# The last four experts of a mixture layer, one by one instead of side by side

## The reference

```python
# mixture: group of 8 experts by argmax, two of its experts, weights from the softmax
weights = p_g * top_p / jnp.sum(top_p, axis=-1, keepdims=True)
...
    a = jax.nn.silu(xb @ w_gate_e[e]) * (xb @ w_up_e[e])     # w_gate_e, w_up_e: 32 x 1024 x 256
    return a @ w_down_e[e]                                     # w_down_e: 32 x 256 x 1024
...
y = yb.reshape(R, D) * row_w[:, None].astype(yb.dtype)
out = jax.ops.segment_sum(y, row_tok, num_segments=T + 1)[:T]
# after it: x = x + out; x = rms_norm(x, final_norm_g), then the second block:
h = rms_norm_2(x, g_pre_mix[i])
q, k, v = split_heads(h, w_qkv)
```

## Time and profile before

| | |
|---|---|
| median of 3 runs | 795.57 us (794.38 to 796.18) |
| profiled execution | 795.36 us, its span 793.6 us |
| TensorE busy | 740.5 us, 93% of the span |
| VectorE busy | 417.3 us, 53% |
| ScalarE busy | 332.8 us, 42% |
| DMA, mean over the span | 257 GB/s, near 420 GB/s in the expert stage |

### The profile page before, as it was taken

How to read it: one execution, slowest core, us unless ns; L and a number is a source line. 1 busy time by engine, 2 the same in 40 slices (tenths; PEclk the granted TensorE clock), 3 DMA queues, 4 the chain that set the end, 5 groups by cost and what they waited for, 6 DMA issues and landing times.

```text
span 793.6 us, 12361 instructions
## 1 busy us (share of the span) xinstructions
PE 740.5 (93%) x5110; PEld 611.7 (77%) x5110; DVE 417.3 (53%) x740; ACT 332.8 (42%) x594; POOL 30.9 (4%) x64
## 2 busy tenths in 40 slices
PE   8999999999999999998776769999998999999996
PEld 8899898888788876665444539899877888888885
DVE  3747756676767421110110107665658776777665
ACT  4667465545444421110110117565556444344442
POOL 0600000000000000000000001000002000000000
PEclk9999999999999999999988989999999999999999
DMA  8765486456978999999999999954433475555201
GB/s 315 273 182 158 146 284 227 171 173 207 371 263 314 341 379 421 420 420 422 421 421 420 421 394 355 374 182 157 145 125 112 151 250 174 170 202 180 87 0 54
DMA packets 83850, 203.97 MB, mean 257 GB/s; under 512 B 6992, under 2 KB 47824, under 8 KB 71248
## 3 DMA queue, kind: packets, MB, share of 16 engines
q1 hardware_dynamic: 83792, 203.15, 69.1%
HBM read 202.09 MB, written 1.05 MB: 256 GB/s over the span
## 4 chain that ended last, share of the span: by engine, by line
PE 80%; DMA 11%; ACT 3%; DVE 3%; SPq 2%; issue 1%; DVEq 0%; ACTq 0%
PE ps L622 44%; PE ps L690 9%; PE ps L953 5%; PE ps L693 5%; DMA big<-in_w_gate_e 4%; DMA ext<-in_w_up_e 3%; DMA raw<-in_w_gate_e 3%; PE ps L974 2%; PE ps L932 2%; PE ps L984 2%; SPq L467 1%; DVE wl L1563 1%; PE ps L585 1%; ACT junk L1191 1%; PE ps L1039 1%
## 5 line engine op out<-in xcount | busy, mean ns | idle before, releaser
L1563 DVE TENSOR_TENSOR wl<-raw,wh 128x1024 fp32r<-128x1024 f32 (+3 forms) x180 | 213.1, 1199 | 130.7 <-ACT wh L1182 129.2
L1182 ACT CAST wh<-raw 128x1024 fp32r<-128x1024 f32 (+3 forms) x180 | 181.8, 1028 | 66.7 <-PE ps L622 46.3
L622 PE MATMUL ps<-wh,fra 128*128 128x512 f32 (+3 forms) x668 | 189.5, 369 | 1.1 <-DVE wl L1563 0.7
L622 PEld LDWEIGHTS ps<-wh,fra 128*128 128x128 f32 x668 | 118.6, 189 | 20.1 <-DVE wl L1563 1.7
L622 PE MATMUL ps<-wl,fra 128*128 128x512 f32 (+3 forms) x334 | 121.3, 363 | 0.0
L690 PE MATMUL ps<-fra,wh 128*128 128x512 f32 x352 | 110.6, 396 | 0.0
L622 PE MATMUL ps<-fra,wh 128*128 128x256 f32 x464 | 86.1, 287 | 1.4 <-DVE big L1984 1.4
L693 PEld LDWEIGHTS ps<-fra,wl 128*128 128x128 f32 x352 | 66.1, 188 | 15.5
L622 PEld LDWEIGHTS ps<-fra,wh 128*128 128x128 f32 x464 | 72.7, 192 | 2.4 <-issue 2.2
L622 PE MATMUL ps<-wh,frb 128*128 128x512 f32 x240 | 74.3, 391 | 0.0
L622 PEld LDWEIGHTS ps<-wl,fra 128*128 128x128 f32 x334 | 62.9, 188 | 9.7
(11 more groups left out here) (245 smaller groups left out, 920.4 us busy)
## 6 DMA issues: line engine op xcount, KB each, us to landing
raw<-in_w_gate_e SPq DMA_DIRECT2D x28, 1024.0 KB, 23.9
ext<-in_w_up_e SPq DMA_DIRECT2D x24, 1024.0 KB, 26.4
raw<-in_w_in SPq DMA_DIRECT2D x16, 1024.0 KB, 5.2
ext<-in_w_down_e SPq DMA_DIRECT2D x16, 1024.0 KB, 24.2
raw<-in_w_qkv SPq DMA_DIRECT2D x12, 1024.0 KB, 12.8
raw<-in_w_gate SPq DMA_DIRECT2D x11, 1024.0 KB, 5.3
raw<-in_w_up SPq DMA_DIRECT2D x11, 1024.0 KB, 5.2
raw<-in_w_down SPq DMA_DIRECT2D x11, 1024.0 KB, 4.9
```

The lines of the kernel that those rows point to most:

```text
L622: t = e.matmul(o, a, w, start=first and n == 0, stop=final and n == 2, skip_group_check=not check)
L1182: e.copy(halves(q)[0], piece_view(q)).then_inc(*up("wh", q))
L1563: e.tensor_tensor(l, piece_view(q), h.bitcast(F), ALU.subtract).then_inc(*up("wl", q))
```

## The change

Group 7 alone is done in another way; groups 0 to 6 are as before.

- The combine weights of group 7 are made and turned during group 6, after its combine (`select_last_weights`, `gather_last_weights`), and lie four times over, once on each 32 partitions, in `CM7`, one tile for each of the four experts.
- Between the gate and the up product of group 7 stand 26 filler products.
- `one_expert(j)` then takes the four experts in turn. Down product: the 32 slots of one expert go to four groups of 32 partitions of one bank, and each group gets another quarter of the 1024 features. ScalarE alone copies the bank (128x256). Combine: eight products, each with 32 rows of the array (one group), into `turned(k)`. After the first three experts stand three filler products; the 12 are gone.
- `combined` for the eight tiles is now raised in the last four products of the last expert.
- The second block's first unit, ("q", 0), is fetched as two units of half a megabyte. The gains, and then the bias table, come one whole unit earlier in the queue.

```diff
-WARM = (15, 3, 12, 9, 14, 4)
+WARM = (15, 3, 3, 9, 14, 4, 26)
...
-            wt.split((key, c), w_qkv[0].rearrange("(k p) n -> p k n", p=P)[:, :, col:col + 256])
+            w = w_qkv[0].rearrange("(k p) n -> p k n", p=P)[:, :, col:col + 256]
+            wt.split((key, c), *((w[:, 0:4], w[:, 4:8]) if (key, c) == ("q", 0) else (w,)))
...
+    last_weighed = big[:, 1280:1792]
...
+    YE7 = [junk[:, 256 * j:256 * j + 256] for j in range(4)]
+    CM7 = [ext[:, 8, 256 * j:256 * j + 256] for j in range(4)]
...
             for half_, key in enumerate(("eg", "eu")):
+                if half_ and g == 7:
+                    warm(WARM[6], 3)
...
-        def experts_down(g):
+        def turn_hidden(g):
             z = g % 2
...
-            if g == 7:
-                warm(WARM[2], 3)
+
+        def experts_down(g):
+            z = g % 2
+            turn_hidden(g)
...
+        def gather_last_weights():
+            for r in range(2):
+                enter(1, "CM", 7, r)
+                e.wait_ge(*at("sel weights", 7, r))
+                for n in range(4):
+                    t = e.transpose(bank[1][:, P * n:P * n + P], last_weighed[:, P * n:P * n + P], ident)
+                t.then_inc(*up("CM turned", 7, r))
+
+        def one_expert(j):
+            b, ed = 2 + j % 2, wt.raws["ed", 28 + j]
+            e.wait_ge(*landed(ed))
+            enter(b, "YE act", 7, j)
+            for k in range(2):
+                for r in range(4):
+                    t = e.matmul(bank[b][32 * r:32 * r + 32, 0:256], AT[1][:, P * k + 32 * j:P * k + 32 * j + 32],
+                                 slot_view(ed)[:, k, 256 * r:256 * r + 256], start=(k == 0), stop=(k == 1))
+            t.then_inc(*(up("taken", "ed", 7) if j == 3 else up("down", 7, j)))
+            e.wait_ge(*at("YE act", 7, j))
+            for s in range(2):
+                for r in range(4):
+                    k, rows = 2 * r + s, slice(32 * r, 32 * r + 32)
+                    t = e.matmul(turned(k), YE7[j][rows, P * s:P * s + P], CM7[j][rows, :], start=False, stop=(j == 3),
+                                 skip_group_check=True)
+                    if j == 3 and s:
+                        t.then_inc(*up("combined", 7, k))
+            if j < 3:
+                warm(WARM[2], 0)
...
             experts(g)
-            gather_weights(g)
             if g < 7:
+                gather_weights(g)
                 gather(g + 1)
-            experts_down(g)
-            combine(g)
+                experts_down(g)
+                combine(g)
+            if g == 6:
+                gather_last_weights()
+        turn_hidden(7)
+        e.wait_ge(*at("AT", 7))
+        for j in range(4):
+            one_expert(j)
...
+            if g == 6:
+                for r in range(2):
+                    e.wait_ge(*at("CM turned", 7, r))
+                    e.copy(ext[:, 8, 512 * r:512 * r + 512], bank[1][:, :]).then_inc(*up("CM", 7, r))
+        for j in range(4):
+            e.wait_ge(*(at("taken", "ed", 7) if j == 3 else at("down", 7, j)))
+            e.copy(YE7[j], bank[2 + j % 2][:, 0:256]).then_inc(*up("YE act", 7, j))
...
+        def select_last_weights():
+
+            e.wait_ge(*at("gathered", 7, 1))
+            slots = C[:, C_IOTA:C_IOTA + CAP].unsqueeze(1).to_broadcast([P, 4, CAP])
+            for r in range(2):
+                e.wait_ge(*(at("CM turned", 7, 0) if r else at("CM turned", 6)))
+                for n in range(4):
+                    j, i = 2 * r + n // 2, n % 2
+                    t = e.tensor_scalar(last_weighed[:, P * n:P * n + P].rearrange("p (e s) -> p e s", e=4), slots,
+                                        PX[:, i, 28 + j:29 + j], kept_W[:, i, 28 + j:29 + j], ALU.is_equal, ALU.mult)
+                t.then_inc(*up("sel weights", 7, r))
```

More of the change, by code:

```diff
@@ L983, in combine @@
                     e.wait_ge(*at(("YE act", "YE dve")[k // 4], g))
-                t = e.matmul(turned(k), YE[k // 4][:, P * (k % 4):P * (k % 4) + P], CM, start=False, stop=(g == 7),
+                t = e.matmul(turned(k), YE[k // 4][:, P * (k % 4):P * (k % 4) + P], CM, start=False, stop=False,
                              skip_group_check=True)
-                if g == 7 and k % 2:
-                    t.then_inc(*up("combined", g, k))
-            if g < 7:
-                t.then_inc(*up("combined", g))
+            t.then_inc(*up("combined", g))
+        def gather_last_weights():
[24 more added lines that the diff above has]
+                warm(WARM[2], 0)
         gather(0)
@@ L1429, in scalar @@
             e.activation(AE[z], bank[0][:, 0:256], ACT.Silu).then_inc(*up("expert silu", g))
-            e.wait_ge(*at("CM turned", g))
-            e.copy(CM, bank[1][:, 0:256]).then_inc(*up("CM", g))
             if g < 7:
+                e.wait_ge(*at("CM turned", g))
+                e.copy(CM, bank[1][:, 0:256]).then_inc(*up("CM", g))
                 gather(g + 1)
@@ L1435, in scalar @@
             e.copy(AT[z], bank[1][:, 0:256]).then_inc(*up("AT", g))
-            e.wait_ge(*at("down", g))
-            e.copy(YE[0], bank[2][:, :]).then_inc(*up("YE act", g))
+            if g < 7:
+                e.wait_ge(*at("down", g))
+                e.copy(YE[0], bank[2][:, :]).then_inc(*up("YE act", g))
+            if g == 6:
[5 more added lines that the diff above has]
+            e.copy(YE7[j], bank[2 + j % 2][:, 0:256]).then_inc(*up("YE act", 7, j))
         if real:
@@ L1958, in vector @@
             e.tensor_tensor(AE[z], AE[z], bank[0][:, 256:512], ALU.mult).then_inc(*up("expert a", g))
+            if g < 6:
+                select_weights(g + 1)
             if g < 7:
-                select_weights(g + 1)
                 gather(g + 1)
-            e.wait_ge(*at("taken", "ed", g))
-            e.tensor_copy(YE[1], bank[3][:, :]).then_inc(*up("YE dve", g))
+                e.wait_ge(*at("taken", "ed", g))
+                e.tensor_copy(YE[1], bank[3][:, :]).then_inc(*up("YE dve", g))
+            if g == 6:
+                select_last_weights()
         if real:
@@ L2107, in general_vector @@
     def general_vector(e):
-        e.wait_ge(*at("YE act", 7))
+        e.wait_ge(*at("YE act", 7, 3))
         e.wait_ge(*at("combined", 7, 7))
```

## The result

The changed kernel took **802.12 us** (median of 4 runs, 799.28 to 803.46) against 795.70 us for the kernel before on the same chip: a ratio of 1.0073, 95% interval 1.0059 to 1.0087, so 0.7% slower. The forecast was slower by 3 us, 798.7 us, range 796.0 to 802.5; the sign and the mechanism hold, the size is about double. The profiled execution took 799.28 us, its span 797.5 us.

The account below looks back on a forecast made before the run. The prediction took as bound when ScalarE can begin the eight high halves. Up product -2.3 us, spent at once; last expert's result +3.6, pacing -0.35: +3.2 us, so 798.7 us, range 796.0 to 802.5.

Parts of the forecast that it names:

- Part 1: Weights of group 7 turned during group 6: added transposes start the gate product 0.5 us later, covered by the fillers.
- Part 2: 26 fillers before group 7's up product keep the clock up: 3.66 instead of 6.23 us, ending 2.2 to 2.3 us earlier.
- Part 3: Group 7's experts one by one: 3.27 us a period against 2.5 us between landings, so high halves start 3.6 us later.
- rival 1: Row tiles of the combine overlap less: 802 us in pairs (chance 0.13), 809 us one by one (0.04).
- Part 4: From high halves to turning back: unpaced copies give 0.35 us back, TensorE's branch costs nothing; turning back 3.2 us later.
- no cost, but no room either: TensorE's jump over the general path, 2.16 us, would end at 481.4 us, just ahead of the second block's first product.
- rival 2: TensorE's clock drops at the fillers or in the one-by-one stretch: up product 2.5 us longer, 801.3 us, chance 0.07.
- Part 5: Second block's first unit in two halves, bias table one unit earlier: both worth nothing.
- Tiles that overlap less: Combine's row tiles run in pairs or one by one: 802 us (chance 0.13) or 809 us (0.04).
- the smaller period: Hand-overs and fillers between experts nearly vanish, 2.5 us a period: 796.4 us, no change, chance 0.11.
- The dropping clock: Fillers before the up product or the one-by-one stretch fail to hold TensorE's clock: 801.3 us, chance 0.07.
- The faster case: Experts keep up with the landings, fourth down product at 471.96 us, high halves at 474.7 us: 793.5 us, chance 0.08.

Follow-up runs that it names:

- e1: The changed kernel run once more, unchanged: 802.28 us, ratio 1.0074 to the kernel before.
- e10: The changed kernel without the 26 filler products ahead of the up product of group 7: 803.25 us, ratio 1.0085.
- e6: The kernel before with 26 filler products ahead of the up product of group 7, nothing else: 795.89 us, ratio 1.0000.
- e3: The changed kernel with eight more filler products right behind the last combine: 800.70 us, ratio 1.0060.
- e8: The changed kernel with the general path for crowded experts, and so its branch, left out on TensorE: 800.92 us, ratio 1.0064.
- e7: The kernel before with the second block's first unit fetched as two halves, unit list otherwise as before: 795.78 us, ratio 0.9998.
- e11: The changed kernel with down products issued ahead of the previous combine, no small fillers, eight at the end, second weight transposes behind the gate product, 23 fillers: 798.07 us.
- e2: The changed kernel without the three filler products after each of the first three experts: 801.06 us, ratio 1.0068.

## Why the prediction was right, and where it was short

Times here are counted as in the table, with the stage's start as before.

**Part 1** (gate product 0.5 us later): 0.71 us in the profiled execution (2.46 us from the first transposes to the gate product, where I had 2.2). But it is 0.7 to 1.7 us from execution to execution. I had taken the idle 1.73 us as room; in the kernel before it also took up how late group 6 ended. After the change nothing does, and the delay is passed on. In e1 it was 1.72 us, and that trace ended 6.5 us late; so this is the larger part of why the median (+6.4 us) lies above the profiled execution (+5.3 us).

**Part 2** held: the up product at 3.66 us with the clock at 1.00 and its end at 465.8 us against 465.6 forecast. The fillers did not end at the landing but followed the late gate product, so their worth is 2.2 us where the gate product is early and about 1 us where it is late (e10). On the kernel before they are worth nothing (e6).

**Part 3**, the deciding step, was right in kind: four row tiles run side by side (16 combine records in 1.15 us, rival 1 gone), the experts fall behind the landings, the fourth sets the end. The term that was mis-sized is the period: **3.50 us, not 3.27**. Down product and hand-over took 1.56 us from start to start (1.04 + 0.58 = 1.62 forecast), the combine 1.08 (0.96), the three fillers with the changes of shape around them 0.86 (0.69). The fourth down product came at 478.3 instead of 477.5 us, the high halves at 481.0 instead of 480.3 us.
The combine took 0.12 us an expert more than I put it, 0.5 us for four. The excess is not in the overlap, since a step of four records took 0.215 us as in the down product; the first step took 0.32 us, which the sum had in it, and 0.32 us passed again from the last step to the first record of another shape behind it, which it had not. The estimate of 1.0 us more by the factor that the Trainium skill gives for four row tiles (TensorE: Matmul & The Clock Gate, Part 3) is not borne out by this trace.

**Part 4** failed in two steps. First, "no cost, but no room either": the branch began at 479.9 us (forecast 479.2, the difference being the later fourth expert), took 2.96 us, not 2.16 as in the one row that I had the earlier trace rows, and held the first product back by 0.5 us. I had treated a duration that had been covered as a constant. Second, the hole behind the last combine: I weighed holes inside the one-by-one stretch (rival 2), but not this one, which my own numbers put at 1.35 us and which became 2.06 us. Behind it the 24 records took 1.5 us longer than in e3. The sum from the forecast of +3.2 us: +0.7 for the high halves, +0.3 for the input, +0.5 for the branch, and +0.6 for the 24 records, which I had given 3.8 us and which took 4.44 us (2.95 in e3), make 5.3 us. The forecast had 5.1 us from the high halves to the turning back, by way of ScalarE, and that was right wherever the clock held (5.12 us in e3, 5.08 in e8); in the changed kernel it was 6.48 us.

**Part 5** held for the split unit (e7). The new order of the gains and the bias table was not run by itself, but in no trace was anything won or lost behind the turning back.

**The rivals.** Tiles that overlap less, and the smaller period, did not occur. The dropping clock did, at a place other than the one I named, and together with the chain rather than instead of it. The faster case needed a fourth down product before 474.2 us. In the changed kernel it came at 478.3; only with the overlap that I had named for it did it come in time (e11: 472.6 us, high halves at 475.62 instead of 476.70), and there the branch took it back. The median lies 0.4 us inside the upper end of my range, which had been set by row tiles in pairs and by a clock that drops elsewhere; that it still lies inside is luck.

## What to carry to other kernels

Serial small steps cost their hand-overs each time; issue the next step's first half ahead of this step's second half, and most of the hand-overs vanish (without small fillers, from the first down product to the fourth: 7.91 us in e2, 5.02 us in e11). Before filling an idle stretch of an engine, ask which jitter it takes up in the executions that were not profiled. The branch on TensorE cost nothing under queued work; where a change removes that cover, do not take one observed duration for it (here 0.37 to 4.59 us), and look for transfers of instructions beside it.

## What the runs showed of the hardware

- The same branch with the same outcome took 0.37 to 4.59 us on TensorE. In the ten long cases it ended 1.40 to 1.55 us after a 16 KB packet on the instruction queue had landed.
- Holes of 2.06, 2.27, 2.39, 2.40, 2.73 and 3.17 us behind the last combine were each followed by TensorE's low clock, those of 0.20, 0.28 and, twice, 1.59 us were not. In another place, behind the fillers in e6, a hole of 2.38 us was not followed by it either. What tells these apart is open.
- Four records on 32 rows of the array each, with 256 columns, ran fully side by side: a step of four every 0.215 us, as one record on 128 rows in the combine of the kernel before. Each change of shape around them cost about 0.1 us more.
